# Turning a recurrent head's decayed keys: TensorE transposes replaced by VectorE 32x32 blocks and a round through DRAM

## The reference, cut to what matters

```python
q_dec = q * jnp.exp(b)
k_dec = k * jnp.exp(b_last - b)
decay = jnp.exp(b_last[:, :, 0])
def step(S, xs):
    qd, kd, vn, dn = xs
    o = jnp.einsum('bthk,bhkv->bthv', qd, S)
    S = dn[..., None] * S + jnp.einsum('bthk,bthv->bhkv', kd, vn)
    return S, o
```

## Time and profile before

| | |
|---|---|
| time, median of 3 runs | 1386.17 us (1385.78 to 1386.58) |
| profiled execution | 1386.22 us, span 1384.4 us |
| TensorE busy | 1369.9 us (99%) |
| VectorE busy | 1046.2 us (76%) |
| ScalarE busy | 837.3 us (60%) |
| POOL busy | 186.0 us (13%) |
| DMA | 140.41 MB, 101 GB/s on average |

### The profile page before, as it was taken

The page is one execution under the profiler, slowest core; times in us unless marked ns, Lnnn a source line. Parts: engine busy times, 40 slices in busy tenths (PEclk is TensorE's granted clock), DMA queues, the critical chain, the costliest instruction groups (busy, mean ns, idle before and its releaser), DMA issues.

```text
span 1384.4 us, 32303 instructions
## 1 busy us (share of the span) xinstructions
PE 1369.9 (99%) x13108; PEld 1291.0 (93%) x13108; DVE 1046.2 (76%) x1765; ACT 837.3 (60%) x1802; POOL 186.0 (13%) x158
## 2 busy tenths in 40 slices
PE   9999999999999999999999999999999999999998
PEld 9999999998999999999998888888888899999987
DVE  6888887788646777877667888888886478888864
ACT  7666666666434666666555667666664456666654
POOL 1111222220000000000001122222210000000100
PEclk9999999999999999999999999999999999999999
DMA  5332322332323333333233232333323233334432
GB/s 188 117 98 93 108 85 86 108 108 78 99 71 122 101 99 100 103 90 100 70 107 108 87 106 85 108 107 108 108 82 108 85 110 107 108 107 114 114 96 76
DMA packets 76340, 140.41 MB, mean 101 GB/s; under 512 B 9504, under 2 KB 39456, under 8 KB 76192
## 3 DMA queue, kind: packets, MB, share of 16 engines
q1 hardware_dynamic: 76192, 138.35, 33.0%
HBM read 112.36 MB, written 17.30 MB: 94 GB/s over the span
## 4 chain that ended last, share of the span: by engine, by line
PE 89%; DVE 5%; ACT 2%; issue 2%; DMA 0%; SPq 0%; DVEq 0%; ACTq 0%
PE proj L1926 64%; PE far L2191 5%; PE pair L2174 3%; PE pair L2176 3%; PE far L2208 2%; PE pair L2059 1%; PE far L2193 1%; PE far L2144 1%; PE far L2145 1%; PE pair L2124 1%; DVE ops L1660 1%; PE pair L1926 1%; PE pair L2131 1%; DVE w_lo L1392 1%; PE far L2148 1%
## 5 line engine op out<-in xcount | busy, mean ns | idle before, releaser
L1926 PE MATMUL proj<-u_hi,w_hi 128*128 128x264 f32 (+1 forms) x1960 | 478.7, 312 | 1.9 <-DVE w_lo L1392 0.7
L1926 PE MATMUL proj<-u_lo,w_hi 128*128 128x264 f32 (+1 forms) x1960 | 458.2, 302 | 0.0
L1926 PE MATMUL proj<-u_hi,w_lo 128*128 128x264 f32 (+1 forms) x1960 | 458.1, 302 | 0.0
L1926 PEld LDWEIGHTS proj<-u_hi,w_hi 128*128 128x128 f32 x1960 | 314.7, 189 | 19.3 <-issue 1.4
L1926 PEld LDWEIGHTS proj<-u_hi,w_lo 128*128 128x128 f32 x1960 | 314.0, 188 | 13.6
L1926 PEld LDWEIGHTS proj<-u_lo,w_hi 128*128 128x128 f32 x1960 | 314.0, 188 | 10.6
L1392 DVE TENSOR_TENSOR w_lo<-w_raw,w_hi 128x1024 fp32r<-128x1024 f32 x178 | 221.9, 1247 | 35.9 <-ACT w_hi L952 35.8
L1200 ACT ACTIVATE decay<-pair,neg_max 128x528 f32<-128x528 f32 (+1 forms) x144 | 100.3, 697 | 203.4 <-DVE neg_max L1782 203.3
L952 ACT ACTIVATE w_hi<-w_raw 128x1024 fp32r<-128x1024 f32 x178 | 186.5, 1048 | 39.4 <-PE proj L1926 36.6
L1782 DVE TENSOR_REDUCE neg_max<-pair 128x1 f32<-128x528 f32 (+1 forms) x144 | 101.4, 704 | 90.5 <-PE pair L2176 89.3
L892 POOL TENSOR_TENSOR mix_lo<-mixed_t,mix_hi 128x528 fp32r<-128x528 f32 (+1 forms) x32 | 50.9, 1590 | 502.0 <-ACT mix_hi L1247 502.0
(11 more groups left out here) (257 smaller groups left out, 2245.7 us busy)
## 6 DMA issues: line engine op xcount, KB each, us to landing
w_raw<-w_units SPq DMA_DIRECT2D x178, 512.0 KB, 3.6
v_scratch<-blocks SPq DMA_DIRECT2D x128, 64.0 KB, 2.1
v_rows<-v_scratch SPq DMA_DIRECT2D x32, 256.0 KB, 2.9
o_scratch<-blocks SPq DMA_DIRECT2D x104, 64.0 KB, 2.7
q_stack<-gate_f SPq DMA_DIRECT2D x32, 132.0 KB, 2.4
k_stack<-k_stack SPq DMA_DIRECT2D x32, 132.0 KB, 2.4
o_rows<-o_scratch SPq DMA_DIRECT2D x14, 256.0 KB, 3.8
ops<-o_scratch SPq DMA_DIRECT2D x12, 256.0 KB, 2.6
```

Of the source, the lines that this page charges most:

```text
L1926: ins = pe.matmul(out, w, x[:, tile, cols_n], start=(k == 0 and p == 0), stop=(k == last_k and p == 2))
```

## The change

For each recurrent head VectorE turns the 512 non-meta tokens of the backward keys (into `blocks`, at step 7) and of the forward keys (into the new `kf_blocks`, at step 8) in 32x32 blocks. SyncE writes both to scratch tensors with four DMAs each (at its step 8) and reads them back into `k_landing`, a part of `q_level`, once the levels are done (at its step 9). ScalarE joins them into `cols` (`join_keys`), at the end of its steps 10 and 11. TensorE keeps the turn of the 16 meta keys only. Its products of the backward keys move from step 10 to step 11, in front of `turn_meta` and the forward products; VectorE's `chain_back`, `gate_meta` and `chain_forward` all stand at step 11; and TensorE's output products at step 12 stand behind the feeding of that step.

```diff
@@ buffers
+        kf_blocks = sb("kf_blocks", [P, N_CHUNKS * P])
+        kb_scratch = nc.dram_tensor("kb_scratch", (P, N_BLOCKS, N_CHUNKS * BLOCK), f32, kind="Internal").ap()
+        kf_scratch = nc.dram_tensor("kf_scratch", (P, N_BLOCKS, N_CHUNKS * BLOCK), f32, kind="Internal").ap()
+        k_landing = tuple(q_level[:, i, 0:SEQ] for i in range(2))
@@ SyncE
+            def write_keys(g, scratch, src, ready, landed, written):
+                sp.wait_ge(ready, g + 1)
+                if g > 0:
+                    sp.wait_ge(landed, 16 * g)
+                for i in range(N_BLOCKS):
+                    sp.dma_start(scratch[:, i, :].rearrange("(j c) x -> c j x", j=N_BLOCKS),
+                                 src[i * BLOCK:(i + 1) * BLOCK, :].rearrange("c (j x) -> c j x", j=N_BLOCKS))\
+                        .then_inc(written, 16)
+            def read_keys(g, dst, scratch, written, landed):
+                sp.wait_ge(written, 16 * N_BLOCKS * (g + 1))
+                sp.wait_ge(levels_done, (g + 1) * GROUPS)
+                sp.dma_start(dst, scratch.rearrange("p i x -> p (i x)")).then_inc(landed, 16)
...
+                        if c < HG_HEADS and s == LEVELS:
+                            write_keys(l * HG_HEADS + c, kb_scratch, blocks, kb_blocked, kb_landed, kb_written)
+                            write_keys(l * HG_HEADS + c, kf_scratch, kf_blocks, kf_blocked, kf_landed, kf_written)
+                        if c < HG_HEADS and s == LEVELS + 1:
+                            read_keys(l * HG_HEADS + c, k_landing[0], kb_scratch, kb_written, kb_landed)
+                            read_keys(l * HG_HEADS + c, k_landing[1], kf_scratch, kf_written, kf_landed)
@@ ScalarE, hgrn
                 if s == TURN_KEYS:
                     copy_v(n)
-                    act.wait_ge(k_turned, 2 * g + 1)
-                    first = first_back(l)
-                    act.activation(cols[:, first:4, :],
-                                   pair[:, 0, first * P:].rearrange("p (c n) -> p c n", c=4 - first),
-                                   ACT.Copy).then_inc(k_ready, 1)
                     copy_far_halves(g)
                     fill_score(g)
                 if s == TURN_KEYS + 1:
-                    act.wait_ge(k_turned, 2 * g + 2)
-                    step(act.activation(cols[:, 4:7, :],
-                                        pair[:, 1, 0:3 * P].rearrange("p (c n) -> p c n", c=3), ACT.Copy))
-                    act.activation(cols[0:N_META, 7, :], meta[0:N_META, 0:P], ACT.Copy)\
-                        .then_inc(k_ready, 1)
+                    act.wait_ge(k_turned, g + 1)
+                    step(act.activation(cols[0:N_META, 7, :], meta[0:N_META, 0:P], ACT.Copy))
...
+            def join_keys(l, g, s):
+                first = first_back(l)
+                if s == TURN_KEYS + 1:
+                    dst, of = cols[:, first:4, :], slice(first, 4)
+                    act.wait_ge(kb_landed, 16 * (g + 1))
+                else:
+                    dst, of = cols[:, 4:7, :], slice(0, 3)
+                    act.wait_ge(kf_landed, 16 * (g + 1))
+                    act.wait_ge(act_step, own[0])
+                landing = k_landing[s - TURN_KEYS - 1].rearrange("p (i h r) -> p h i r", i=N_BLOCKS, r=BLOCK)
+                act.activation(dst.rearrange("p h (i r) -> p h i r", r=BLOCK), landing[:, of, :, :], ACT.Copy)\
+                    .then_inc(k_ready, 1)
@@ ScalarE, the list
                         for i in units_raised(c, s):
                             raise_next(l * LAYER_UNITS + i)
+                        if c < HG_HEADS and s in (TURN_KEYS + 1, TURN_KEYS + 2):
+                            join_keys(l, l * HG_HEADS + c, s)
@@ VectorE
+            def block_keys(l, c, first):
+                n, g = l * HEADS + c, l * HG_HEADS + c
+                dve.wait_ge(k_widened, TURNS * (g + 1))
...
+                dst, done = (blocks, kb_blocked) if first == KB else (kf_blocks, kf_blocked)
+                dve.transpose(dst[:, :].rearrange("p (j h r) -> p h j r", j=N_BLOCKS, r=BLOCK),
+                              ops[:, c % 2, first, N_META:T].rearrange("p (h j c) -> p h j c", h=N_CHUNKS, c=BLOCK))\
+                    .then_inc(done, 1)
...
                     if lv < TURNS:
                         total_pairs(lv + 1)
+                    if s == TURNS:
+                        block_keys(l, c, KB)
+                    elif s == LEVELS:
+                        block_keys(l, c, KF)
...
-                elif s == TURN_KEYS + 1:
+                elif s == TURN_KEYS + 2:
                     chain_back(l, g)
-                elif s == TURN_KEYS + 2:
-                    chain_forward(g)
                     if c > 0:
                         gate_meta(l, c - 1)
+                    chain_forward(g)
@@ TensorE
                     turn_v(l, c)
-                    pe.wait_ge(k_widened, (g + 1) * TURNS)
-                    pe.wait_ge(blended, g * BLENDS + 4)
-                    for j in range(first_back(l), N_CHUNKS):
-                        ins = pe.transpose(pair[:, 0, j * P:(j + 1) * P], ops[:, c % 2, KB, chunk(j)],
-                                           ident[:, :])
-                    ins.then_inc(k_turned, 1)
...
                 elif s == TURN_KEYS + 1:
-                    pe.wait_ge(blended, (g + 1) * BLENDS)
-                    pe.wait_ge(far_halves, 2 * (g + 1))
-                    for j in range(N_CHUNKS - 1):
-                        pe.transpose(pair[:, 1, j * P:(j + 1) * P], ops[:, c % 2, KF, chunk(j)], ident[:, :])
+                    pe.wait_ge(k_widened, (g + 1) * TURNS)
                     pe.wait_ge(v_ready, n + 1)
                     pe.transpose(meta[0:N_META, 0:P], ops[:, c % 2, KF, 0:N_META], ident[:, :])\
                         .then_inc(k_turned, 1)
+                elif s == TURN_KEYS + 2:
+                    pe.wait_ge(blended, g * BLENDS + 4)
                     pe.wait_ge(k_ready, 2 * g + 1)
                     pe.wait_ge(v_landed, 16 * (n + 1))
...
                     ins.then_inc(kv_done, 1)
-                elif s == TURN_KEYS + 2:
+                    if c > 0:
+                        turn_meta(n - 1)
+                    pe.wait_ge(blended, (g + 1) * BLENDS)
+                    pe.wait_ge(far_halves, 2 * (g + 1))
                     pe.wait_ge(k_ready, 2 * g + 2)
...
                     ins.then_inc(kv_done, 1)
-                    if c > 0:
-                        turn_meta(n - 1)
...
                     for s in range(steps_of(c)):
+                        if c < HG_HEADS and s == HG_STEPS - 1:
+                            feed(l, c, s)
+                            hgrn(l, c, s)
+                            continue
                         (hgrn if c < HG_HEADS else attend)(l, c, s)
                         feed(l, c, s)
```

More of the change, by code:

```diff
@@ L515, in encoder_trunk @@
         k_ready = sem("k_ready")
+        kb_blocked = sem("kb_blocked")
+        kb_written = sem("kb_written")
+        kb_landed = sem("kb_landed")
+        kf_blocked = sem("kf_blocked")
+        kf_written = sem("kf_written")
+        kf_landed = sem("kf_landed")
         kv_done = sem("kv_done")
@@ L1467, in block_values @@
                     dve.wait_ge(o_written, 16 * N_BLOCKS * rounds_before(n - 1))
+                if 0 < c <= HG_HEADS:
+                    dve.wait_ge(kb_written, 16 * N_BLOCKS * (l * HG_HEADS + c))
                 dve.transpose(blocks[:, :].rearrange("p (j h r) -> p h j r", j=N_BLOCKS, r=BLOCK),
```

6 lines of the change are left out of this document (added).

## The result

The changed kernel takes **1485.7 us** (median of 4 runs, 1482.6 to 1487.5) against 1386.17: **7.1% slower**, ratio 1.0714, interval 1.0702 to 1.0727. The profiled execution has a span of 1485.7 us, 101.3 longer than that of before (1384.4). Among all executions reported here one ran at a granted clock of 0.654 from end to end (1974.65 us, of the kernel "filled, first form"), and no reading rests on it.

A forecast was written before the change was run, and what follows sets the result against it. TensorE, busy 99% of the span, was taken as the bound. Net losses of 40.6 us (layer 0, heads 1 to 7), 23 (layer 1) and 2 (first heads) sum to 65.7 on 1386.17: 1452 us, range 1412 to 1488.

The forecast's parts named there:

- my first case: Recurrent heads: TensorE waits before the backward and the forward products, both as worked out; 1452 us, chance 0.56.
- my third: TensorE's clock falls around the waits, costing each of 14 heads 1.8 to 3.5 us; 1477 to 1501 us, chance 0.20.
- My own sign against the first case: TensorE: matmuls after the waits running at twice their time would show that the clock falls.
- Removed: TensorE: 104 transposes at 0.11 us are 11.4 us; with 2.8 us of idle time, best case 14.2 us gained.
- First wait: TensorE before the backward products, for keys through DRAM: 2.8 us a head in layer 0, 2.7 in layer 1.
- The two legs: Backward keys' round through DRAM: 4.1 us for the four writes, 2.9 us for the read back to land.
- Second wait: TensorE before the forward products, their join behind `round_mixed` in ScalarE's list: 3.8 us a head in layer 0, 1.3 in layer 1.
- Costs of nothing: VectorE's 1.4 us more a head, SyncE's ten more DMAs a head and 16 x 1 MB of traffic, all taken as covered.
- Load ahead of the writes: SyncE's step 7 weight load, ahead of the key writes, waits for VectorE's low cut; its issue takes 0.43 us.

The follow-up runs named there:

- filled, first form: Changed kernel with matmuls of ones by ones, results unread, put into TensorE's two waits for the keys in each recurrent head (9, then 15 or 4): 1467.61 us, ratio 1.0582.
- the filled kernel: Changed kernel with unread matmuls of the identity and `v_rows` put into TensorE's two waits in each recurrent head (8, then 13 or 3): 1465.66 us, ratio 1.0573.

## Why the prediction was right, and where it fell short

The prediction was 1452 us; the kernel takes 1485.7, which is in the range (1412 to 1488), 2.3 us below its upper end, and it is slower, as forecast with 0.91. What happened is not my first case alone but my third, which had 0.20: the waits as worked out, and the clock on top. My own sign against the first case came: behind the waits the matmuls start about twice as far apart. That the range holds all the same is partly luck, as it ends in the middle of the third case.

- **Removed.** 11.4 us forecast, about 9 to 11 measured (0.086 to 0.107 each against 0.11).
- **First wait.** 2.8 us a head in layer 0 forecast, 2.0 to 2.2 measured in heads 1 to 6; 2.7 in layer 1, and 1.6 to 2.75 measured in the same heads. The two legs are right: 4.1 for the writes (4.17 in head 5), 2.9 for the read (2.74). The rule of some 2 us a trip, which the Trainium skill gives in "DMA: Bandwidth & Descriptors", section "Latency and other measured facts", would have hidden it: by the trace the way from the first write to the start of the join was 6.9 us. A single landing is not far from that rule (medians of 2.8 us for a backward write of 64 KB and 2.7 for its read of 256 KB); what comes on top is the issue of eight writes one after another, 3.8 us, ahead of the read.
- **Second wait.** 3.8 us forecast, 3.5 to 3.6 measured in layer 0; 1.3 and 1.0 to 1.3 in heads 1 to 5 of layer 1. The join drawn ahead took 22 of the 33 us away, so its cause is shown and not only its size.
- **Together.** My terms give (2.8 + 3.8) x 7 + (2.7 + 1.3) x 7 + 2 = 76.2 us of waits; the profile has 42.8 + 32.6 = 75.4. That close a fit is in part luck: head 7, which I took to be of the same size, waits 6.4 + 2.6 us in layer 0 and 5.8 and nothing in layer 1, more than my 6.6 and 4.0. Head 0, taken as 1 us, waits 2.6 and 3.5. Heads 1 to 6 wait less: 34 us in layer 0 and 20 in layer 1 where my terms give 40 and 24. Head 7's excess is ScalarE's list behind VectorE's late blend, by the trace.
- **What failed** is the step from the rivals to the number. Rival 3 gave 1.8 to 3.5 us a head for the clock, 25 to 49 in all, and some 37 us came, in all 16 heads. The waits that I forecast in case 1 are just its condition, so with case 1 at 0.56 the clock's term belonged in the sum, not beside it with 0.20. The rows that I held against each other spoke for it: the first matmuls after idle time ran at half the pace, and I had seen nothing that made a wait of 3.8 us different. The sum with the term, 65.7 + 37, is 1489. The Trainium skill's page "TensorE: Matmul & The Clock Gate" says in the section "Why this matters for your kernels" that gaps between bursts bring the lower clock back; by the 421 ns against 275 and the filled kernel the trace agrees.
- **Costs of nothing.** VectorE's 19.8 us more (1046.2 to 1066.0) and the traffic: no run isolates them. The kernel with the forward keys alone bounds their part of it: its 18.3 us of span are 18.7 of idle time in front of waits already named, and TensorE's busy time is only 0.4 us lower where 48 transposes less should give 4 to 5. So some 4 us at most are left there for slower matmuls and contention together.
- **Load ahead of the writes:** taken as 0.43 us of issue. The run with the writes early puts it at 14 us in all, 7.8 of it wait.

No version beats the kernel before. The best with both keys through DRAM is 1428 us, with the forward ones alone 1403. The two gains that were run apart (feeding ahead of the products, and the load behind the reads) were not run together, so it stays open how low that comes; each alone left over 50 us of idle time.

## What to carry to other kernels

Where an engine that bounds the kernel is to wait where it never waited, price its clock with the wait: here 75 us of waits in pieces of 0.4 to 6.4 us, mostly two a head with 1 us of work between them, cost some 37 us more of slower matmuls. Work that is worth 0.1 us an instruction on the bound engine pays for no trip whose result is needed within 7 us: look first for how long before its use the operand exists, and only then at what the trip removes. And a wait that is one engine's order (a join queued behind an unrelated rounding) is the cheap one to find and mend: it was 33 us for two lines, and the same look at head 7 was left undone.

## What the runs showed of the hardware

- TensorE's granted clock was 0.91 over the stretch with the waits of heads 1 to 6 of layer 0, with waits of 2.2 and 3.6 us a head around 1 us of work, between its levels of 1.2 and 2.4 GHz; with the same gaps filled it was 0.98. In head 5 it was 1.00 in the backward products, half in the second wait and the forward products, and 0.99 again some eight matmuls of the projection later.
- A short single wait did not bring it down: with the forward keys alone, one wait a head and of at most 2.0 us in heads 0 to 6, the forward products took 275 ns. Only behind the waits of 4.4 and 4.2 us of the two heads 7 they took 421 ns (mean of all 293, clock 0.996).
- A 256 KB read from DRAM issued 0.55 us behind a 512 KB load in the same queue was there 4.5 us after its own issue, and after 2.6 us with the load behind it (medians of 16 reads to the landing: 3.9 and 2.7 us).
- With the filling TensorE's own work took 33.6 us less, and its time without own work grew by 15.0 us: read as above, what a faster engine gains is partly lost again where an arrival is fixed by others.
